# Two mixers and an MLP on one core: rotary products moved from GpSimd to VectorE, gates by tanh at later places, attention values beside the next scores, and four groups of unread transposes

## The chip, the cores and the metric

The kernel runs on one core of a Trainium2 chip. The metric is the device time of one execution in microseconds (us); lower is better. The engines are named as in the profile: PE (TensorE, with its weight loads as PEld), DVE (VectorE), ACT (ScalarE), POOL (GpSimd) and SP (the queue that issues the weight transfers).

## The reference, cut to what matters

Everything is float32, 256 tokens of width 2048. Two blocks follow one another.

```python
# first block
u = rms_norm(h, norm_mix_w);  z = u @ w_in           # 2048 x 11264
y_a = rms_norm(hgrn2_scan(...), hg_norm_w) * silu(hg)
y_b = chunk_band_attention(aq, ak, av, rel_bias)     # 16 heads of 64
merged = sigmoid(gates_a) * (y_a @ w_branch_a) + sigmoid(gates_b) * (y_b @ w_branch_b)
h = h + merged @ w_out
h = h + square(relu(rms_norm(h, norm_mlp_w) @ w_up)) @ w_down
# second block, 16 meta tokens ahead of the 256
qa, ka, va, ga, qb, kb, vb, gb = split(rmsnorm(h) @ w_in_2)   # 2048 x 6656
ya = attention(rope(rmsnorm(qa)), rope(rmsnorm(ka)), va) * silu(ga)      # 8 heads of 128
yb = rmsnorm(softmax(s1) @ vb - lam * softmax(s2) @ vb, sub_g) * (1 - lambda_init) * silu(gb)
h = h + rmsnorm(concat(ya, yb) @ w_out_2, post_norm_g)
```

`rope(x)` is `x * cos + turned(x) * sin`, per head.

## The kernel before, in words

Every projection is a stream of **chunks**: a chunk is 256 rows by 512 columns of a weight matrix. SP brings it into `raw` (four slots), ACT copies it rounded into `whi` (`split_hi`, L857), DVE writes the rest into `wlo` (`split_lo`, L1240), and PE multiplies it in three products, high by high, high by low, low by high. In the transposed form (`chunk_t`, L430) that is 24 matmuls of 256 columns, in the natural form (`chunk_n`, L442) 12 of 512. Eight chunks (k = 0 to 7) make one **group** of 512 output columns: `g` counts the 22 groups of the first projection, `j` the 13 of the second mixer's. Two sets of PSUM banks (banks 0-1 and 2-3) alternate between groups; banks 4 to 7 are for everything else.

All orders are written out by hand. Each engine has its own loop over the same chunks, and what is called "side work" here is inserted behind chunk k of group g. In the loops of ACT and DVE the place (g, k) begins with the split of chunk k+4, which waits until PE has finished chunk k, so these two engines enter place (g, k) when PE leaves chunk k. Each engine works strictly in its written order: an instruction that waits holds all that stand behind it, the splits included.

The places that the change touches:

- **First attention** (from `G_ATT` = 16). Eight pairs of heads, one every `PAIR_STEP` = 5 chunks: `att_scores` at the pair's place (PE L570, L572), exponentials one chunk later on ACT (L975), their inverse and product on DVE two chunks later (L1448), `att_turn` four chunks later (six transposes, PE L578), `att_copy` on ACT (L982), and `att_values` six chunks later (PE L589, L591). Pair j+1's scores stand at five.
- **HGRN output** (group `G_HGOUT` = 14): four copies on ACT at k = 2 to 5, four squares on POOL, `hg_squares` on PE behind k = 6 (L556), `hg_root` on ACT at k = 7.
- **First gates** (g = 14 to 21): at the end of the group DVE scales the PSUM set into `gates` (L1369) and ACT, at the end of its own group, waits for that and applies Sigmoid (L938).
- **Second mixer.** `rope_squares` (PE L696), `rope_root` (ACT), `rope_turn_halves` (PE L706), `rope_sin` (DVE L1588) for n = 0, 1, 2, and then `rope` on POOL: times cos, plus the sine part, times the inverse root (L1882, L1885, L1888). Units of attention run one per chunk from j = 6 on (place `pos` = 8(j-6)+k): `scores`, `weights_turn` three places later (L745), `values` four later (L758). For the gate groups (j = 9 to 12) DVE scales the set (L1619), ACT applies Sigmoid (L1105), and DVE, which waits for it, multiplies (L1621); POOL later multiplies this into the attention's output (L1902, L1909).

## Time and profile before

| | |
|---|---|
| median of 3 runs | 1920.42 us (1920.09 to 1922.02) |
| the profiled execution | 1919.19 us, its span 1917.4 us |
| PE busy | 1889.7 us, 99% of the span |
| DVE, ACT, POOL busy | 1101.7, 914.2, 178.9 us |
| granted TensorE clock, mean | 0.997 |
| the chain that ended last | PE 94%, DVE 3%, ACT 2%, issue 1% |

The span is measured from the first to the last instruction; 1.8 us of the execution lie around it. PE's matmuls overlap one another in the records, so its busy share says nothing of its speed: what counts is the time from one matmul's start to the next one's start, and the places where PE idles. A row of the chain gives start, length, engine, what is written, line and number of instructions; dividing length by number in a long row gives that distance.

### The profile page before, as it was taken

What the parts mean: (1) busy time and instruction counts of PE and PEld (TensorE: products, weight loads), DVE (VectorE), ACT (ScalarE), POOL (GpSimd) and SP (SyncE); (2) the same over time, 40 slices, a digit from 0 to 9 for tenths busy, and PEclk for the clock granted to TensorE, in tenths of its full rate; (3) what the DMA queues carried; (4) which work ended last, traced back from release to release, by engine and by line L of the source; (5) the groups of instructions that cost most, each with busy time, mean ns of one, the idle gap of its engine ahead of it and who ended that gap; (6) DMA issues with size and microseconds to landing.
All of it is one profiled execution on the core that took longest, in us unless ns stands there. A gap on an engine that the chain in (4) does not pass through costs nothing.

```text
span 1917.4 us, 33984 instructions
## 1 busy us (share of the span) xinstructions
PE 1889.7 (99%) x13468; PEld 1752.5 (91%) x13468; DVE 1101.7 (57%) x1265; ACT 914.2 (48%) x1189; POOL 178.9 (9%) x135
## 2 busy tenths in 40 slices
PE   9999999999999999999999999999999999998998
PEld 9989998999999889988998899899889998888986
DVE  6655766466655555554545545554566457766664
ACT  6534444565644455443443344344454354655543
POOL 2001331401000100000010000000010000031000
PEclk9999999999999999999999999999999999999999
DMA  8665656566565656666656666566555554444454
GB/s 272 191 180 171 185 179 177 152 193 177 171 220 186 208 187 177 196 199 189 196 187 198 190 195 194 190 183 202 188 185 173 175 170 133 116 136 144 133 187 143
DMA packets 176435, 346.49 MB, mean 181 GB/s; under 512 B 10976, under 2 KB 11184, under 8 KB 175776
## 3 DMA queue, kind: packets, MB, share of 16 engines
q1 hardware_dynamic: 174176, 337.76, 57.0%
q0 software_dynamic: 2128, 6.82, 1.4%
q8 instruction: 102, 1.67, 0.3%
q14 instruction: 29, 0.24, 0.0%
HBM read 342.44 MB, written 2.10 MB: 180 GB/s over the span
## 4 chain that ended last, share of the span: by engine, by line
PE 94%; DVE 3%; ACT 2%; issue 1%; DMA 0%; SPq 0%; POOL 0%; DVEq 0%; ACTq 0%
PE ps L430 56%; PE ps L442 32%; DVE wlo L1240 1%; ACT whi L857 1%; PE ps L758 1%; PE ps L527 1%; PE ps L745 1%; PE ps L722 0%; PE ps L460 0%; DMA x_nat<-in_x_dram 0%; PE ps L733 0%; PE ps L578 0%; PE ps L696 0%; DVE p L1652 0%; PE ps L570 0%
## 5 line engine op out<-in xcount | busy, mean ns | idle before, releaser
L1240 DVE TENSOR_TENSOR wlo<-raw,whi 128x1024 fp32r<-128x1024 f32 x631 | 804.1, 1280 | 719.3 <-ACT whi L857 718.3
L857 ACT ACTIVATE whi<-raw 128x1024 fp32r<-128x1024 f32 x631 | 664.1, 1058 | 872.6 <-PE ps L430 545.1
L430 PE MATMUL ps<-xhi,whi 128*128 128x256 f32 (+1 forms) x1984 | 567.3, 286 | 0.0
L430 PE MATMUL ps<-xhi,wlo 128*128 128x256 f32 (+1 forms) x1984 | 555.4, 280 | 0.0
L430 PE MATMUL ps<-xlo,whi 128*128 128x256 f32 (+1 forms) x1952 | 546.8, 280 | 0.0
L430 PEld LDWEIGHTS ps<-xhi,whi 128*128 128x128 f32 x1984 | 375.0, 189 | 10.0 <-issue 7.6
L430 PEld LDWEIGHTS ps<-xhi,wlo 128*128 128x128 f32 x1984 | 373.8, 188 | 0.0
L430 PEld LDWEIGHTS ps<-xlo,whi 128*128 128x128 f32 x1952 | 368.8, 189 | 1.5 <-issue 0.7
L430 PE MATMUL ps<-x2hi,whi 128*128 128x256 f32 x1024 | 282.8, 276 | 0.0
L430 PE MATMUL ps<-x2lo,whi 128*128 128x256 f32 x1024 | 282.7, 276 | 0.0
L430 PE MATMUL ps<-x2hi,wlo 128*128 128x256 f32 x1024 | 282.7, 276 | 0.0
L430 PEld LDWEIGHTS ps<-x2lo,whi 128*128 128x128 f32 x1024 | 192.2, 188 | 0.2
L430 PEld LDWEIGHTS ps<-x2hi,whi 128*128 128x128 f32 x1024 | 192.2, 188 | 0.2
L430 PEld LDWEIGHTS ps<-x2hi,wlo 128*128 128x128 f32 x1024 | 192.2, 188 | 0.0
L442 PE MATMUL ps<-whi,xlo 128*128 128x512 f32 x256 | 100.8, 394 | 0.0
L442 PE MATMUL ps<-whi,ya_lo 128*128 128x512 f32 x256 | 100.8, 394 | 0.0
L442 PE MATMUL ps<-whi,yb_lo 128*128 128x512 f32 x256 | 100.8, 394 | 0.0
L442 PE MATMUL ps<-whi,xhi 128*128 128x512 f32 x256 | 100.8, 394 | 0.0
L442 PE MATMUL ps<-wlo,ya_hi 128*128 128x512 f32 x256 | 100.3, 392 | 0.0
L442 PE MATMUL ps<-wlo,xhi 128*128 128x512 f32 x256 | 100.2, 392 | 0.0
L442 PE MATMUL ps<-wlo,yb_hi 128*128 128x512 f32 x256 | 100.2, 392 | 0.0
L442 PE MATMUL ps<-whi,ya_hi 128*128 128x512 f32 x256 | 99.7, 390 | 0.0
(357 smaller groups left out, 2220.6 us busy)
## 6 DMA issues: line engine op xcount, KB each, us to landing
raw<-in_w_in_dram SPq DMA_DIRECT2D x279, 512.0 KB, 3.8
raw<-in_w_up_dram SPq DMA_DIRECT2D x128, 512.0 KB, 3.8
raw<-in_w_down_dram SPq DMA_DIRECT2D x128, 512.0 KB, 3.7
raw<-in_w_out_dram SPq DMA_DIRECT2D x64, 512.0 KB, 4.0
raw<-in_w_branch_a_dram SPq DMA_DIRECT2D x16, 512.0 KB, 4.2
raw<-in_w_branch_b_dram SPq DMA_DIRECT2D x16, 512.0 KB, 4.1
x_nat<-in_x_dram SPq DMA_DIRECT2D x4, 512.0 KB, 7.0
rel<-in_rel_turned_dram POOLq DMA_DIRECT2D x8, 256.0 KB, 4.4
```

The lines of the kernel that those rows point to most:

```text
L430: ins = mm(outs[b], w[:, k % SLOTS, j, cols], v, start=start, stop=last and j == CK - 1 and i == 2, skip_group_check=True)
L442: ins = mm(ps[:, 2 * s + t, :], v[:, kt, toks], w[:, k % SLOTS, j, :], start=first and j == 0 and i == 0, stop=last and j == CK - 1 and i ...
L527: ins = mm(misc[:, hd // 4, (hd % 4) * P:(hd % 4 + 1) * P], k_both[:, hd, :], spread(qp[:, hd, 0:1], *both_tiles), start=True, stop=True)
L745: ins = nc.tensor.transpose(ps[:, 6, i * P:(i + 1) * P], p[:, i * P:(i + 1) * P], ident[:])
L758: ins = mm(ps[:, 7, 0:P], l, r, start=i == 0, stop=i == 2)
L857: f(whi[:, k % SLOTS], raw[:, k % SLOTS], ACT.Copy).then_inc(whi_ready, 1)
L1240: tt(wlo[:, k % SLOTS], raw[:, k % SLOTS], whi[:, k % SLOTS], ALU.subtract).then_inc(wlo_ready, 1)
```

## The change

It does five things.

1. First attention: `att_values` moves from six chunks behind its scores to five, directly ahead of the next pair's scores.
2. The gates of both mixers use tanh in place of the sigmoid (sigmoid(x) = (1 + tanh(x/2))/2; the factors of a half go into instructions that exist). In the first mixer `gate_tanh` stands on ACT at k = 2 of the next group. In the second, DVE only scales at the group's end and does the rest (`gate_out`) at k = 3 of the next group. `subg` moves from the gate into the copies behind `b_turn`.
3. `rope` and the products of gate and output move from POOL to DVE, each step at a place of its own (`ROPE_STEPS`). POOL keeps nothing in the second mixer but a memset and a DMA.
4. Some places move by one chunk: `hg_squares` and `hg_root`, `values_turn` and its copies, the third rope's squares and turn, `b_turn`.
5. `shift_phase`: three 128x128 transposes whose output nobody reads, at four places: behind (g = 15, k = 2), behind the last `att_values` (g = 21, k = 0), and at pos 20 and 30 of the second mixer.

```diff
+ROPE_FROM = (41, 65, 74)
+ROPE_STEPS = ((45, 54, 56, 58), (69, 70, 71, 71), (78, 85, 86, 87))
-POS_BT = 26
+POS_BT = 27
@@ PE
+            def shift_phase(bank, rows):
+                for i in range(3):
+                    nc.tensor.transpose(ps[:, bank, i * P:(i + 1) * P], rows(i), ident[:])
...
-                    if k == 6 and g == G_HGOUT:
+                    if k == 7 and g == G_HGOUT:
                         hg_squares()
+                    if k == 2 and g == G_HGOUT + 1:
+                        pe.wait_ge(hg_sd, 4)
+                        shift_phase(4, lambda i: acc[:, i, :])
                     at = NC * (g - G_ATT) + k
-                    for part, late in ((att_values, 6), (att_turn, 4), (att_scores, 0)):
+                    for part, late in ((att_values, 5), (att_turn, 4), (att_scores, 0)):
                         if pair_at(at - late) is not None:
                             part(pair_at(at - late))
+                    if at == PAIR_STEP * (AH // 2):
+                        shift_phase(5, lambda i: prob[:, 0, i * P:(i + 1) * P])
...
+                if pos in (POS_B + B_UNITS + 3, POS_BT + 3):
+                    if pos == POS_BT + 3:
+                        pe.wait_ge(bn_copied[0], 2)
+                        pe.wait_ge(bn_copied[1], 2)
+                    shift_phase(6, lambda i: kb[:, 4 * (i % 2), 0:P])
@@ ACT, first mixer
-                elif g >= 14:
-                    act.wait_ge(set_free[s], g // 2 + 1)
-                    v = gates[:, 4 * (g - 14):4 * (g - 14) + 4, :]
-                    f(v, v, ACT.Sigmoid).then_inc(gate_done, 1)
+            def gate_tanh(g):
+                act.wait_ge(set_free[g % 2], g // 2 + 1)
+                v = gates[:, 4 * (g - 14):4 * (g - 14) + 4, :]
+                f(v, v, ACT.Tanh, scale=0.5).then_inc(gate_done, 1)
...
+                    if g >= 15 and k == 2:
+                        gate_tanh(g - 1)
@@ DVE, branches: three instructions keep their number
-                tt(part_a[:], pset(0), gates[:, bass.ds(4 * n, 4), :], ALU.mult).then_inc(set_free[0], 1)
+                stt(out=part_a[:], in0=gates[:, bass.ds(4 * n, 4), :], scalar=1.0, in1=pset(0), op0=ALU.add,
+                    op1=ALU.mult).then_inc(set_free[0], 1)
@@ DVE, second mixer
+            def rope(n, step):
+                s = ROPE_SETS[n]
+                w = TM if n == 0 else T
+                nb = 2 if n == 0 else 4
+                v, r, q = qg[:, 0:nb, 0:w], qrot[:, 0:nb, 0:w], qsq[:, 0:nb, 0:w]
+                if step == 0:
+                    dve.wait_ge(nr_rot, n + 1)
+                    src = ps[:, 2 * s:2 * s + 2, 0:TM] if n == 0 else pset(s)
+                    tt(r, src, spread(sin_t[:], [0, nb], [1, w]), ALU.mult).then_inc(set_free[s], 1)
+                if step == 1:
+                    own(tt(v, v, spread(cos_t[:], [0, nb], [1, w]), ALU.mult))
+                if step == 2:
+                    dve.wait_ge(set_free[s], rope_free[n])
+                    own(tt(v, v, r, ALU.add))
+                if step == 3:
+                    dve.wait_ge(nr_rs, n + 1)
+                    tt(ka[:] if n == 0 else qa[:, 4 * (n - 1):4 * n, :], v, q, ALU.mult).then_inc(nr_done, 1)
...
-                tt(dst, pset(s), rows(4, T), ALU.mult).then_inc(g_raw, 1)
+                stt(out=dst, in0=pset(s), scalar=0.5, in1=rows(4, T), op0=ALU.mult, op1=ALU.mult).then_inc(g_raw, 1)
+                if j == G_IN2 - 1:
+                    gate_out(j)
+            def gate_out(j):
...
                 dve.wait_ge(e_sig, N_E1 + g + 1)
-                stt(out=dst, in0=pset(s), scalar=subg[:] if g < 2 else 1.0, in1=dst, op0=ALU.mult,
-                    op1=ALU.mult).then_inc(set_free[s], 1)
+                stt(out=dst, in0=pset(s), scalar=1.0, in1=dst, op0=ALU.add, op1=ALU.mult).then_inc(set_free[s], 1)
+                y, done = (ob, bn_y) if g < 2 else (oa, an_y)
...
+                tt(y[:, half, :], y[:, half, :], dst, ALU.mult).then_inc(done, 1)
...
+                    if j >= 10 and k == 3:
+                        gate_out(j - 1)
@@ POOL: rope(0), rope(1), rope(2) and the four products with ob and oa are gone
```

**PE at one place of the first attention.** Ahead of these rows and behind them stand matmuls of L430. Before, a pair's scores are followed by a whole chunk and only then come the values of the pair ahead:

```order
L570 MATMUL ps<-ak,aq 128x256 x2
L572 MATMUL ps<-ak,aq 128x128 x2
L430 MATMUL ps<-xhi,whi 128x256
...
L430 MATMUL ps<-xhi,wlo 128x256
L589 MATMUL ps<-prob_t,av 64x256 x2
L591 MATMUL ps<-prob_t,av 64x128 x2
L430 MATMUL ps<-xhi,whi 128x256
```

Now (L596 and L598 are the values, L577 and L579 the scores):

```order
L596 MATMUL ps<-prob_t,av 64x256 x2
L598 MATMUL ps<-prob_t,av 64x128 x2
L577 MATMUL ps<-ak,aq 128x256 x2
L579 MATMUL ps<-ak,aq 128x128 x2
```

The values have moved up by one chunk, so PE leaves and enters the stream of chunks twice per pair instead of three times.

**ACT from the third to the fourth pair.** L857 is the split, L938 the gate, L975 the exponentials, L982 the copies. Before:

```order
L982 ACTIVATE prob_t<-ps 128x384 x2
L857 ACTIVATE whi<-raw 128x1024
L938 ACT_TABLE_LOAD
L938 ACTIVATE gates<-gates 128x1024
L857 ACTIVATE whi<-raw 128x1024
L975 ACT_TABLE_LOAD
L975 ACTIVATE prob,rsum<-prob,nm 128x128
L975 ACTIVATE prob,rsum<-prob,nm 128x256
```

The same stretch now (L874 the split, L1001 the copies, L994 the exponentials, L957 the gate):

```order
L1001 ACTIVATE prob_t<-ps 128x384 x2
L874 ACTIVATE whi<-raw 128x1024 x2
L994 ACTIVATE prob,rsum<-prob,nm 128x128
L994 ACTIVATE prob,rsum<-prob,nm 128x256
L994 ACTIVATE prob,rsum<-prob,nm 128x128
L994 ACTIVATE prob,rsum<-prob,nm 128x256
L1005 ACTIVATE yb_hi<-ps 128x256
L874 ACTIVATE whi<-raw 128x1024 x2
L957 ACTIVATE gates<-gates 128x1024
```

The gate has left the place between two splits ahead of the exponentials, and both table loads are gone. Over the whole program ACT has 17 table loads in place of 36.

**DVE at pos 39, the last place of group j = 10, in the second mixer.** Before, L1637 is the maximum of a unit and L1619, L1621 the gate:

```order
L1637 TENSOR_REDUCE nm<-ps 128x1
L1638 TENSOR_SCALAR nm<-nm 128x1
L1619 TENSOR_TENSOR gb<-ps,row_s 128x1024
L1621 SCALAR_TENSOR_TENSOR gb<-ps,subg,gb 128x1024
L1240 TENSOR_TENSOR wlo<-raw,whi 128x1024
```

Now L1688 is the maximum, L1624 the last step of the third rope, L1655 the gate's scaling, L1262 the split:

```order
L1688 TENSOR_REDUCE nm<-ps 128x1
L1689 TENSOR_SCALAR nm<-nm 128x1
L1624 TENSOR_TENSOR qa<-qg,qsq 128x1024
L1655 SCALAR_TENSOR_TENSOR gb<-ps,row_s 128x1024
L1262 TENSOR_TENSOR wlo<-raw,whi 128x1024
```

The instruction that waited for ACT is gone from here, and a rope step stands ahead of the one that ACT waits for.

## Rows read from the trace of the kernel before

**Rows 1.** Waits of PE, whole run: us in total, times, longest us:

```profile
PE ps L745 <- DVE p L1652: 6.9, 3, 4.5
...
PE ps L578 <- DVE prob L1448: 2.0, 1, 2.0
PE ps L696 <- ACT qsq L1098: 1.8, 1, 1.8
PE ps L570 <- ACT prob_t L982: 1.2, 2, 1.1
PE ps L684 <- DVE v_meta L1580: 1.2, 1, 1.2
...
PE ps L556 <- POOL o_hg L1845: 1.0, 1, 1.0
...
PE ps L758 <- DVE oa L1658: 0.9, 2, 0.5
```

**Rows 2.** Timeline of ACT, first attention: start us, us, instruction, idle before:

```profile
453.46 1.06 ACT L938 ACTIVATE gates<-gates 128x1024 f32<-128x1024 f32 x1 [4.46 <-DVE gates L1369]
...
455.48 1.28 ACT L975 ACT_TABLE_LOAD   x1
```

**Rows 3.** Chain that ended last, 396 to 472 us: start us, us, what:

```profile
461.83 1.56 PE ps L578 x6
463.39 3.79 PE ps L430 x24
```

**Rows 4.** The same chain over the whole run and from 520 us:

```profile
521.96 8.68 PE ps L430 x72
...
531.30 5.46 PE ps L430 x48
...
537.56 107.61 PE ps L430 x912
...
912.12 87.07 PE ps L430 x768
```

**Rows 5.** Timeline of PE around one `att_values`:

```profile
415.80 0.28 PE L430 MATMUL ps<-xhi,wlo 128*128 128x256 f32 x1
416.01 0.65 PE L589 MATMUL ps<-prob_t,av 128*64 128x256 f32 x4
...
416.81 0.38 PE L430 MATMUL ps<-xhi,whi 128*128 128x256 f32 x1
417.03 0.28 PE L430 MATMUL ps<-xlo,whi 128*128 128x256 f32 x1
```

**Rows 6.** Timeline of PE, three transposes between two chunks:

```profile
1812.49 0.49 PE L745 MATMUL ps<-ident,p 128*128 128x128 f32 x3
...
1812.93 0.28 PE L430 MATMUL ps<-xlo,whi 128*128 128x256 f32 x1
```

**Rows 7.** Timelines of DVE, POOL and ACT, 1679 to 1740 us:

```profile
1717.79 1.22 DVE L1588 TENSOR_TENSOR qrot<-ps,sin_t 128x1024 f32<-128x1024 f32 x1
1719.48 6.50 DVE L1240 TENSOR_TENSOR wlo<-raw,whi 128x1024 fp32r<-128x1024 f32 x2 [0.47 <-ACT whi L857]
...
1721.63 3.27 POOL L1888 TENSOR_TENSOR qa<-qg,qsq 128x1024 f32<-128x1024 f32 x1
...
1727.69 1.03 ACT L1105 ACTIVATE ps<-gb 128x1024 f32<-128x1024 f32 x1 [4.11 <-DVE gb L1619]
```

**Rows 8.** Chain that ended last, 1560 to 1822 us:

```profile
1736.55 3.81 PE ps L430 x24
...
1809.82 2.83 PE ps L430 x24
1812.98 2.83 PE ps L430 x24
```

**Rows 9.** Timeline of DVE, 1755 to 1770 us:

```profile
1765.00 2.06 DVE L1652 TENSOR_SCALAR p<-p,rinv 128x272 f32<-128x272 f32 x1
```

**Rows 10.** Busy us (x instructions) of PE, PEld, DVE, ACT, POOL in one stretch:

```profile
1720.00:1822.00 102.00, 94.17 (x764) 91.80 (x762) 65.40 (x113) 52.60 (x84) 14.95 (x6) 0.98 0.45 139
```

More of the change, by code:

```diff
@@ L276, in program @@
         vt_t, vt_c = [sem("vt_t0"), sem("vt_t1")], [sem("vt_c0"), sem("vt_c1")]
-        nr_ev, nr_ss, nr_sd, nr_rs, nr_rot, nr_sin, nr_cos, nr_done = [sem(n) for n in (
-            "nr_ev", "nr_ss", "nr_sd", "nr_rs", "nr_rot", "nr_sin", "nr_cos", "nr_done")]
+        nr_ev, nr_ss, nr_sd, nr_rs, nr_rot, nr_done = [sem(n) for n in (
+            "nr_ev", "nr_ss", "nr_sd", "nr_rs", "nr_rot", "nr_done")]
         u_s, u_nm, u_exp, u_p, u_t, u_pt, u_pv, u_o = [sem(n) for n in (
@@ L817, in _ @@
                     chunk_t(c0, k, CK * k, xh, xl, outs, TM if kv else T, k == 0, k == NC - 1, shared=not kv)
-                    if j == 5 and 2 <= k <= 6:
-                        values_turn(2 * (k - 2))
-                        values_turn(2 * (k - 2) + 1)
-                    for n, jn in enumerate((5, 8, 9)):
-                        if j == jn and k == 1:
+                    if j == 5 and k >= 3:
+                        values_turn(2 * (k - 3))
+                        values_turn(2 * (k - 3) + 1)
+                    for n, first in enumerate(ROPE_FROM):
+                        if NC * j + k == first:
                             rope_squares(n, ROPE_SETS[n])
-                        if j == jn and k == 4:
+                        if NC * j + k == first + 3:
                             rope_turn_halves(n, ROPE_SETS[n])
@@ L1004, in _ @@
                         hg_copy(k - 2)
-                    if g == G_HGOUT and k == 7:
+                    if g == G_HGOUT + 1 and k == 0:
                         for i in range(4):
@@ L1021, in _ @@
                 evac_in(g)
+            gate_tanh(G_IN - 1)
             with act.Fori(0, 4) as n:
@@ L1027, in _ @@
                 act.wait_ge(br_m, n + 1)
-                f(uhi[:, bass.ds(4 * n, 4), :], both[:], ACT.Copy).then_inc(br_hi, 1)
+                f(uhi[:, bass.ds(4 * n, 4), :], both[:], ACT.Copy, scale=0.5).then_inc(br_hi, 1)
             def h_squares(n, free, done, into):
@@ L1104, in evac_in2 @@
                     act.wait_ge(g_raw, g + 1)
-                    f(pset(set_of(j)), dst[:, 4 * (g % 2):4 * (g % 2) + 4, :], ACT.Sigmoid).then_inc(e_sig, 1)
+                    f(pset(set_of(j)), dst[:, 4 * (g % 2):4 * (g % 2) + 4, :], ACT.Tanh).then_inc(e_sig, 1)
             def values_copy(b):
@@ L1159, in side @@
                     f(ob[:, 4 * i:4 * i + 2, :], ps[:, 4 + 2 * i, :].rearrange("p (x c) -> p x c", x=2),
-                      ACT.Copy).then_inc(bn_copied[0], 1)
+                      ACT.Copy, scale=subg[:]).then_inc(bn_copied[0], 1)
             def y_upper(mixer, i, src, ready, done):
@@ L1188, in _ @@
                             f(uhi[:, kt, :], xhi[:, kt, 0:T], ACT.Copy).then_inc(hi_packed, 1)
-                    if j == 5 and 3 <= k <= 7:
-                        values_copy(2 * (k - 3) + 1)
+                    if 4 <= NC * (j - 5) + k <= 8:
+                        values_copy(2 * (NC * (j - 5) + k - 4) + 1)
                     if j >= J_B:
                         side(NC * (j - J_B) + k)
-                    for n, jn in enumerate((5, 8, 9)):
-                        if j == jn and k == 2:
+                    for n, first in enumerate(ROPE_FROM):
+                        if NC * j + k == first + 1:
                             rope_root(n, ROPE_SETS[n])
@@ L1580, in values_copy @@
                 nc.vector.tensor_copy(v_meta[0:META, b, :], ps[0:META, 4 + b % 4, T:T + P]).then_inc(vt_c[0], 1)
[L1582 to L1588 removed]
+            rope_free = (SETS_BEFORE_2 + 4, need2[7] + 1, need2[8] + 1)
+            def rope(n, step):
[15 more added lines that the diff above has]
+                    tt(ka[:] if n == 0 else qa[:, 4 * (n - 1):4 * n, :], v, q, ALU.mult).then_inc(nr_done, 1)
             def rows(n, w):
@@ L1675, in b_norm @@
                     dve.wait_ge(bn_t, i + 1)
-                    nc.vector.tensor_copy(ob[:, 4 * i + 2:4 * i + 4, :],
-                                          ps[:, 5 + 2 * i, :].rearrange("p (x c) -> p x c", x=2)).then_inc(bn_copied[1], 1)
+                    ts(ob[:, 4 * i + 2:4 * i + 4, :], ps[:, 5 + 2 * i, :].rearrange("p (x c) -> p x c", x=2), subg[:],
+                       None, ALU.mult).then_inc(bn_copied[1], 1)
             def side(pos):
@@ L1713, in _ @@
                             nc.vector.tensor_copy(dst, xlo[:, kt, 0:T]).then_inc(lo_packed, 1)
-                    if j == 5 and 3 <= k <= 7:
-                        values_copy(2 * (k - 3))
-                    for n, jn in enumerate((5, 8, 9)):
-                        if j == jn and k == 5:
-                            rope_sin(n, ROPE_SETS[n])
+                    if 4 <= NC * (j - 5) + k <= 8:
+                        values_copy(2 * (NC * (j - 5) + k - 4))
                     if j >= J_B:
                         side(NC * (j - J_B) + k)
+                    for n, places in enumerate(ROPE_STEPS):
+                        for step, place in enumerate(places):
+                            if NC * j + k == place:
+                                rope(n, step)
+                    if j >= 10 and k == 3:
+                        gate_out(j - 1)
                     if j == G_IN2 - 1 and k in (2, 4):
```

51 lines of the change are left out of this document (13 added, 38 removed).

## The prediction

> **What bounds the kernel now.** I read the page first. PE is busy for 99% of the span, and the chain is 94% PE. The chip is not waiting for weights: the waits of PE name no transfer after the start. So time can come only from PE: from where it idles, or from how closely its matmuls follow one another.
>
> For the first I read the waits of PE [rows 1]. Look at the totals: DVE's `p` 6.9 us, `prob` 2.0, ACT's `qsq` 1.8, `prob_t` 1.2, `v_meta` 1.2, POOL's square 1.0, `oa` 0.9. Together that is 15.0 us in eleven waits, all around attention side work that this change touches.
>
> For the second I read long rows of the chain [rows 4]. The same 256-column matmul of L430 comes every 87.07/768 = 113.4 ns in the MLP, but every 107.61/912 = 118.0 ns from 537.56 us on, with nothing between the matmuls and no wait. PE thus has two distances for one instruction, 4.6 ns apart, and keeps one for a hundred microseconds. In the short rows the distance changes at side work: 8.68/72 = 120.6 ns behind an `att_values` (entry included), 5.46/48 = 113.8 ns behind the next six transposes. I call them the close and the wide distance.
>
> Then I read why ACT and DVE are late. In the timeline of ACT [rows 2] the gate at 453.46 us stood idle for 4.46 us: ACT had reached its group's end and waited for DVE to scale the last sums. Behind it on ACT stand a split, a table load of 1.28 us and the pair's exponentials; DVE's product waits for these, and PE's six transposes for DVE. The second mixer has the same figure at its gate groups [rows 7]: ACT idle 4.11 us ahead of its sigmoid. There DVE is held too: two splits take 6.50 us where one such instruction alone takes 1.22 us, while POOL's rope is at work (3.27 us for one product). At 1765.00 us a product of 272 columns takes 2.06 us [rows 9] while POOL multiplies.
>
> **The change part by part.**
>
> *HGRN squares one chunk later.* PE waited 1.0 us for POOL's fourth square [rows 1]. A chunk is 24 x 113.4 ns = 2.7 us, more than the wait, so it goes: **-1.0**. `hg_root` then has two more chunks before the first unread transposes wait for it.
>
> *First gates.* `gate_tanh` at k = 2 finds the scaling long done; it no longer stands between the split and the exponentials at a group's end, and the order shows no table load. Both waits of the first attention, 1.2 and 2.0 us, go. The 2.0 us wait had a wake: its six transposes took 1.56 us [rows 3], against some 0.11 us each elsewhere, so 0.9 us more; and the chunk behind took 3.79 us in place of 2.7, 1.1 us more. **-5.2** in all. ACT gives up 19 table loads, which cover nothing on the path besides. What is late next: the exponentials of one pair now share their place with a gate (at = 26), 1.06 us more on ACT, with more than two chunks until PE asks; nothing.
> The Trainium skill ("ScalarE: Activation LUTs", *Table sets: the hidden batching unit*) puts exp and tanh in one set, and its section *What ACT_TABLE_LOAD costs* asks about 2.7 us for each switch with its drain. The row shows 1.28 us and no drain; by the page's figure the loads would weigh twice as much, which changes no term, since only the waits count.
>
> *Values beside the next scores.* Going from the stream to `att_values` took 416.01 - 415.80 = 0.21 us, and from its first matmul behind to the second 417.03 - 416.81 = 0.22 us [rows 5], each 0.113 us in the stream. One entry and one exit less per pair saves 0.10 + 0.11 = 0.2 us, seven times: **-1.4**. The values now wait for copies made one chunk earlier; the scores at that place wait for the same copies already, so no new wait.
> Six stretches of three chunks behind values run wide, as the row at 521.96 us does [rows 4], at 72 x 4.6 ns = 0.33 us each; a seventh is the long one below. Behind scores the same chain mostly runs close. With scores last at the shared place: **-1.9** (bounds 0 to -2.0).
>
> *Unread transposes.* Three of them between two chunks: from the first to the second matmul behind is 1812.93 - 1812.49 = 0.44 us [rows 6], less 0.11 that belongs to the stream, so 0.33 us each time, 1.3 us for four. That is certain. What they return is a matter of the distance. At the second place stand the 912 matmuls at the wide distance: 912 x 4.6 ns = 4.2 us. The trace shows six transposes of `prob` against the identity, the same instruction, turning wide into close (8.68/72 to 5.46/48, [rows 4]). It also shows three of `p` turning nothing: 2.83 us per 24 ahead and behind [rows 8]. I take the first, because at this place they follow other side work and read the same tile: **-4.2 + 0.3**. At the first place six chunks remain to be turned, 0.7 - 0.3: **-0.3**. At the two places in the second mixer a handful of chunks: 0 (from +0.7 to -0.7).
>
> *Values' transposes.* They and their copies move a chunk away from `rope_root`, which with two table loads held ACT: **-1.2**, the whole wait for `v_meta`.
>
> *Third rope a chunk later, second rope on DVE ahead of the scaling.* PE waited 1.8 us for the squares of `qg`, behind DVE and POOL. DVE now does three steps of 1.22 us [rows 7] at 70 and 71, the scaling follows, and PE asks one chunk later: **-1.8**.
>
> *Gate groups of the second mixer.* The wait of 4.5 us (of 6.9) has POOL's hold on DVE, the wait for the sigmoid and the table load in its chain. Gone, DVE leaves the end of the group some 4 us earlier. The chunk behind it took 3.81 us in place of 2.83 [rows 8]: 1.0 more. I leave 0.2 us for what stays: **-5.3**. The other waits at the two later boundaries are 6.9 - 4.5 = 2.4 and 0.9 us. At one of them (j = 10) a rope step of 1.22 us now stands ahead of the scaling for which ACT waits, so I leave 1.2 us there: **-2.1**.
> DVE receives nine rope steps and four products, 13 instructions; those from 1720 us on are three and four of 1.22 us, 8.5 us. DVE was busy for 65.4 of those 102 us [rows 10]: they fit, and POOL's hold goes.
>
> *At nothing:* the branch products and `subg` (an instruction of the same size for another, on engines with idle time); `b_turn` a chunk later (nobody asks until pos 31).
>
> Sum: 1.0 + 5.2 + 1.4 + 1.9 + 3.9 + 0.3 + 1.2 + 1.8 + 5.3 + 2.1 = 24.1 us. The profiled execution took 1919.2 us, 1.2 below the median of 1920.4, and its waits are what I took away; 1920.4 - 24.1 = **1896.3 us**.
>
> **The rivals.**
>
> *The transposes turn nothing at the second place.* For it: the three of `p` above. Then the 4.2 us stay: 1900.5 us.
> The Trainium skill ("TensorE: Matmul & The Clock Gate", *Wait — 56ns, not 53.3ns?*) gives a warm matmul one distance, its columns over 2.4 GHz and a fixed 2.5 ns; by it no transpose could change anything. Two distances for one shape in the rows contradict it.
>
> *The waits move.* DVE holds more, and ACT still waits for its scaling at each group's end. If half of what the second mixer's gate groups and ropes give (1.8 + 5.3 + 2.1 = 9.2, so 4.6) comes back as waits of L758 and L745, it is 1900.9 us. Against it: DVE's idle third.
>
> *Slower: the wrong distance for the rest.* The distance persists. Every group of transposes ahead of the MLP left the close one in this trace, but if the new history leaves the wide one, 3,072 matmuls of `x2` and 960 of the second projection lose 4.6 ns each, 18.5 us, the 1,536 of 512 columns some 7 us at the same step, and the 4.2 us stay: 1896.3 + 29.7 = 1926 us. It decides once more than 24.1 us, some 5,200 matmuls, run wide. Eight transposes ahead of the MLP stand unchanged, so I hold it for unlikely.
>
> *No effect.* Waits return in full and the transposes fail: around 1919 us.
>
> **How the numbers follow.** The sum 0.54; transposes turn nothing 0.26; waits move 0.12; no effect 0.04; slower 0.04. The likeliest case has a range of its own from 1892 (the second mixer's wide chunks turn as well, no wait is left) to 1899. For 8 in 10 I take 1890 to 1903: it holds the first three cases but for their tails. A measurement of this kernel can tell about 0.2%, 3.8 us, from no change: faster 0.92, same 0.04, slower 0.04.
>
> **What would show it.** In the chain after, the row of 912 or so matmuls before the output projection should be near 103.4 us, not 107.6. The waits of PE should have no `prob`, `prob_t`, `qsq`, `v_meta` and no 4.5 us; L745 and L758 together below 2 us. ACT's idle ahead of the first gates should be gone, POOL idle from 1570 us. In the first attention no chunk should take 3.8 us. Wrong it would be by new waits of `nm`, or of a set that the gate frees three chunks later, or by long rows of 118 ns where there were 113.4.

## The result, and the profile after

The changed kernel took 1899.83 us (median of 4 runs, 1897.56 to 1900.73), the kernel before on the same chip 1920.26 us. The ratio is 0.9894, with a 95% interval from 0.9882 to 0.9906: 1.1% faster. The forecast was 1896.3 us, from 1890 to 1903. The profiled execution took 1897.56 us with a span of 1895.8, at a granted clock of 0.999.

I read the waits of PE first. Each row is an engine and line, what it waited for, the total in us, how often, and the longest:

```profile
PE ps L490 <- DMA mix_rows<-in_norm_mix_w_dram: 3.0, 1, 3.0
PE ps L770 <- DVE oa L1709: 1.8, 2, 1.5
PE ps L475 <- DMA x_nat<-in_x_dram: 0.9, 2, 0.7
PE ps L734 <- DVE nm L1686: 0.6, 2, 0.5
```

Against [rows 1], `p`, `prob`, `prob_t`, `qsq`, `o_hg` are gone and `v_meta` has 0.2 us left. What grew is the wait of the values for `oa`, with 1.5 us at the boundary behind group j = 10. (Line numbers are new: the stream's L430 and L442 are now L432 and L444, scores L577 and L579, values L596 and L598, the first mixer's turn L585, the unread transposes L495, the second mixer's values L770, the splits L874 and L1262.)

Then the chain, at one pair of the first attention, at the second place of the unread transposes, and at the output projection (start, us, what, instructions):

```profile
425.45 0.66 PE ps L585 x6
426.11 2.74 PE ps L432 x24
428.85 0.58 PE ps L596 x4
429.43 0.22 PE ps L598 x4
429.65 0.63 PE ps L577 x4
430.28 0.22 PE ps L579 x4
430.50 11.51 PE ps L432 x96
...
528.97 0.48 PE ps L495 x3
529.45 106.09 PE ps L432 x936
...
1800.29 87.91 PE ps L444 x384
```

Here is both the part that came out as forecast and the part that did not. The long row is now at 106.09/936 = 113.3 ns, the close distance, where [rows 4] had 118.0. But the 96 matmuls behind the shared place of values and scores take 11.51/96 = 119.9 ns with their exit: all four chunks wide. I had expected them close.

ACT's timeline around the fourth gate, the one that [rows 2] shows before:

```profile
455.83 1.06 ACT L874 ACTIVATE whi<-raw 128x1024 fp32r<-128x1024 f32 x1 [1.62 <-PE ps L432]
456.79 1.04 ACT L957 ACTIVATE gates<-gates 128x1024 f32<-128x1024 f32 x1
458.66 1.06 ACT L874 ACTIVATE whi<-raw 128x1024 fp32r<-128x1024 f32 x1 [0.82 <-PE ps L432]
459.62 0.85 ACT L1001 ACTIVATE prob_t<-ps 128x384 f32<-128x384 f32 x2
```

The gate stands right behind a split, with no idle time ahead of it and no table load behind.

To place the gains I took, in each trace, the time from the first matmul of one chunk to the first of a later one. Chunks are counted through the program: 112 to 119 is g = 14, 120 to 175 are the groups of the first attention and the one ahead, 176 to 239 the branches and their output, 240 the MLP, and j = 0 of the second mixer begins at 496. The last row runs from chunk 600 to the end of the span. These sums are worked out from the starts of the traces' matmuls, in us; they serve for the experiments too.

```
chunks              before changed  e12     e1      e3      e4      e6      e11
0-40   start        113.65  114.70  113.76  113.86  114.92  116.39  116.78  113.60
112-120 (squares)    31.96   30.19   30.19   30.19   30.19   31.96   30.19   30.19
120-176 (attention) 183.20  177.72  177.72  178.17  177.45  177.99  175.97  176.25
176-240 (branches)  181.57  177.60  177.60  181.57  177.60  181.57  177.60  177.60
240-536             825.73  825.73  825.97  825.74  825.74  825.75  825.73  825.74
536-552 (j=5,6)      60.73   59.78   59.60   59.58   59.59   61.16   59.61   59.67
568-576 (j=9)        30.05   28.22   28.21   28.22   28.58   30.34   28.22   28.21
576-584 (j=10)       36.31   29.54   29.54   29.55   29.54   35.96   29.54   29.53
584-592 (j=11)       34.60   34.20   34.31   34.20   34.20   34.69   34.29   33.00
592-600 (j=12)       29.65   28.10   28.09   28.10   28.30   29.63   28.30   28.30
600-632 (output)     95.64   95.65   95.65   95.66   97.35   95.64   97.36   97.36
```

Between the first two columns the sum of the gains is 21.6 us: 1.8 at the squares, 5.5 in the attention, 4.0 in the branches, 1.0 at j = 5 and 6, 10.6 from j = 9 to 12, and 1.1 lost at the start, where nothing was changed. Of the 1.8 at the squares 0.4 come back in chunk 120, just behind that row: the squares stand a chunk later now, and the chunk behind them takes 3.23 us in place of 2.83. So they gave 1.4, and the attention 5.9.

### The profile page after: what moved, and what is told of

Same layout as the page of the kernel before. It is cut to its first block, busy times and chain, and to the rows that moved or that the text cites. A ratio compares the mean times of both kernels' runs of the same rounds, so it can differ in the third digit from the quotient of the medians.

```text
span 1895.8 us, 33990 instructions
## 1 busy us (share of the span) xinstructions
PE 1881.1 (99%) x13480; PEld 1746.7 (92%) x13480; DVE 1102.9 (58%) x1278; ACT 888.8 (47%) x1170; POOL 143.5 (8%) x122
## 4 chain that ended last, share of the span: by engine, by line
PE 98%; DVE 1%; ACT 0%; DMA 0%; issue 0%; SPq 0%; DVEq 0%; ACTq 0%
PE ps L432 59%; PE ps L444 32%; PE ps L770 1%; PE ps L534 1%; PE ps L734 1%; PE ps L757 0%; ACT whi L874 0%; DVE wlo L1262 0%; PE ps L462 0%; DMA x_nat<-in_x_dram 0%; PE ps L745 0%; PE ps L585 0%; PE ps L577 0%; PE ps L596 0%; PE ps L718 0%
## 5 line engine op out<-in xcount | busy, mean ns | idle before, releaser
L1262 DVE TENSOR_TENSOR wlo<-raw,whi 128x1024 fp32r<-128x1024 f32 x631 | 796.7, 1269 | 699.2 <-ACT whi L874 698.2
L874 ACT ACTIVATE whi<-raw 128x1024 fp32r<-128x1024 f32 x631 | 664.5, 1058 | 888.9 <-PE ps L432 561.7
L432 PE MATMUL ps<-xhi,whi 128*128 128x256 f32 (+1 forms) x1984 | 565.5, 285 | 0.2
L432 PE MATMUL ps<-xhi,wlo 128*128 128x256 f32 (+1 forms) x1984 | 554.8, 280 | 0.0
L432 PE MATMUL ps<-xlo,whi 128*128 128x256 f32 (+1 forms) x1952 | 546.0, 280 | 0.0
L432 PEld LDWEIGHTS ps<-xhi,whi 128*128 128x128 f32 x1984 | 374.2, 189 | 9.1 <-issue 6.5
L432 PEld LDWEIGHTS ps<-xhi,wlo 128*128 128x128 f32 x1984 | 372.8, 188 | 0.0
L432 PEld LDWEIGHTS ps<-xlo,whi 128*128 128x128 f32 x1952 | 367.5, 188 | 1.4 <-issue 0.7
L432 PE MATMUL ps<-x2hi,whi 128*128 128x256 f32 x1024 | 282.8, 276 | 0.0
L432 PE MATMUL ps<-x2lo,whi 128*128 128x256 f32 x1024 | 282.7, 276 | 0.0
L432 PE MATMUL ps<-x2hi,wlo 128*128 128x256 f32 x1024 | 282.7, 276 | 0.0
L432 PEld LDWEIGHTS ps<-x2lo,whi 128*128 128x128 f32 x1024 | 192.2, 188 | 0.2
L432 PEld LDWEIGHTS ps<-x2hi,whi 128*128 128x128 f32 x1024 | 192.2, 188 | 0.2
L432 PEld LDWEIGHTS ps<-x2hi,wlo 128*128 128x128 f32 x1024 | 192.2, 188 | 0.0
L444 PE MATMUL ps<-whi,ya_lo 128*128 128x512 f32 x256 | 100.8, 394 | 0.0
L444 PE MATMUL ps<-whi,yb_lo 128*128 128x512 f32 x256 | 100.8, 394 | 0.0
L444 PE MATMUL ps<-whi,xlo 128*128 128x512 f32 x256 | 100.8, 394 | 0.0
L444 PE MATMUL ps<-wlo,ya_hi 128*128 128x512 f32 x256 | 100.3, 392 | 0.0
L444 PE MATMUL ps<-wlo,yb_hi 128*128 128x512 f32 x256 | 100.2, 392 | 0.0
L444 PE MATMUL ps<-whi,xhi 128*128 128x512 f32 x256 | 100.2, 391 | 0.0
L444 PE MATMUL ps<-wlo,xhi 128*128 128x512 f32 x256 | 100.1, 391 | 0.0
L444 PE MATMUL ps<-whi,ya_hi 128*128 128x512 f32 x256 | 99.7, 390 | 0.0
```

The costliest lines, as they stand in the source:

```text
L432: ins = mm(outs[b], w[:, k % SLOTS, j, cols], v, start=start, stop=last and j == CK - 1 and i == 2, skip_group_check=True)
L444: ins = mm(ps[:, 2 * s + t, :], v[:, kt, toks], w[:, k % SLOTS, j, :], start=first and j == 0 and i == 0, stop=last and j == CK - 1 and i ...
L874: f(whi[:, k % SLOTS], raw[:, k % SLOTS], ACT.Copy).then_inc(whi_ready, 1)
L1262: tt(wlo[:, k % SLOTS], raw[:, k % SLOTS], whi[:, k % SLOTS], ALU.subtract).then_inc(wlo_ready, 1)
```

## The experiments

Twelve experiments follow, the last of them the changed kernel again. All times are medians of four or five runs each, and the kernel before was measured on the same chip: 1921.56 us for e1 to e4, 1920.62 for e5 to e8, 1920.37 for e9 to e12. Runs of one kernel spread over 1 to 5 us, of which e12 shows a part, so small effects are read from stretches of the trace and not from medians.

**e1: no unread transposes at the second place.**

```diff
-                    if at == PAIR_STEP * (AH // 2):
-                        shift_phase(5, lambda i: prob[:, 0, i * P:(i + 1) * P])
```

> The changed kernel without the three unread transposes at the second place (behind the last pair of the first attention); the other three places stay. Theory (PE keeps one of two distances between matmuls until side work turns it): the row of some 936 matmuls of L432 from about 529 us takes 118.0 ns each, 110.4 us, in place of 113.35 ns and 106.1 us, and may leave at the same stage; against the changed kernel 4.3 us more less 0.3 us for the three transposes, so +3.9 us, about 1903.7 us at the median. Rival (the distance came from something else in the new order, such as scores last at the shared place): the row stays at 113.4 ns and the kernel takes 0.3 us less, about 1899.5 us.

Measured: 1902.38 us (1901.08 to 1903.43), 0.9901 of before (0.9886 to 0.9916). The chain:

```profile
528.25 110.44 PE ps L432 x936
```

The same 936 matmuls take 118.0 ns each. The first mixer's end (120 to 240) is 4.4 us longer than in the changed kernel, three transposes saved included. Nothing else in the program differs. The theory holds: three unread transposes of some 0.3 us are worth 4.4 us. It holds in all fourteen traces: chunks 176 to 240 take 177.60 us in the ten with these transposes and 181.57 us in the four without. Whether another small piece of work there, or a pause of that length, would turn the distance as well was not tried. The MLP behind is close in both, so the harm ends at the next groups of side work.

**e2: none of the twelve.**

```diff
-                    if k == 2 and g == G_HGOUT + 1:
-                        pe.wait_ge(hg_sd, 4)
-                        shift_phase(4, lambda i: acc[:, i, :])
...
-                    if at == PAIR_STEP * (AH // 2):
-                        shift_phase(5, lambda i: prob[:, 0, i * P:(i + 1) * P])
...
-                if pos in (POS_B + B_UNITS + 3, POS_BT + 3):
...
-                    shift_phase(6, lambda i: kb[:, 4 * (i % 2), 0:P])
```

> The changed kernel with none of the twelve unread transposes. Theory: the first place turned nothing (-0.3 us), the second is worth 3.9 us net, the third turned the two to five chunks around the second rope (24 matmuls each at 4.6 ns, 0.2 to 0.6 us, about its own cost of 0.3), the fourth costs 0.3: together about +3.6 us against the changed kernel, 1903.4 us. Rival (none of them matters): 12 transposes of 0.11 us less, 1898.5 us. If the distance behind the whole mixer changes with the history, the long rows of the MLP would show 118 ns and the time would be tens of us more; the row of 3,072 tells that.

Measured: 1904.83 us (1901.15 to 1905.88), 0.9905 (0.9890 to 0.9921). Chunks 120 to 240 took 359.41 us against 359.74 in e1: the first place returned nothing there and cost its own 0.33. But around the third place the chain has this, with no transposes near:

```profile
1678.04 16.39 PE ps L432 x144
```

In the changed kernel the row at this place was 16.40 us for 144, close as well, and I had given the third place the credit. In e3, with the transposes in place, it took 16.96 us. So at the third place they decided nothing that these traces show. At the fourth they cost nothing: without them PE waits for `qrot`, and the chunk behind takes 3.77 us for 3.52.

**e3: values back in a gap of their own.**

```diff
-                    for part, late in ((att_values, 5), (att_turn, 4), (att_scores, 0)):
+                    for part, late in ((att_values, 6), (att_turn, 4), (att_scores, 0)):
...
-                    if at == PAIR_STEP * (AH // 2):
+                    if at == PAIR_STEP * (AH // 2) + 1:
```

> The changed kernel with each pair's values back six chunks behind (in the gap by themselves, one chunk after the next pair's scores), the unread transposes of the second place one chunk later with them. My prediction valued the shared place at 3.3 us (1.4 for entries and exits, 1.9 for wide stretches that turn close). After the trace of the changed kernel my theory is that a pair of stretches there runs wide all four chunks, 16.56 us a pair against 16.65 us: the shared place gives about 0.1 us a pair, so this version takes 0.8 us more than the changed kernel, about 1900.6 us, with the stretch behind scores close (113.4 ns) and that behind values wide (119 to 120 ns). Rival (the shared place gives what was predicted and something else, such as the tanh gates, took it back): +3.3 us, 1903.1 us, and chunks behind the tanh gate longer than their neighbours.

Measured: 1899.41 us (1898.12 to 1899.95), 0.9882 (0.9867 to 0.9897). One pair of its chain:

```profile
432.62 8.68 PE ps L432 x72
441.30 0.66 PE ps L585 x6
441.95 2.74 PE ps L432 x24
444.69 0.63 PE ps L577 x4
445.33 0.22 PE ps L579 x4
445.55 2.92 PE ps L432 x24
448.47 0.58 PE ps L596 x4
449.05 0.22 PE ps L598 x4
449.27 0.79 PE ps L432 x5
```

A pair takes 449.27 - 432.62 = 16.65 us against 16.55 of the changed kernel (430.50 to 447.05 in its chain). The shared place saves an entry and an exit (0.2 us) and pays with a fourth wide chunk (0.1 us): 0.1 us a pair, some 0.7 us in all, where I had put 3.3. By the medians the two kernels can't be told apart. Part of e3's good time is not of its edit: the transposes of the first place, the same in both and ahead of it, left the close distance here (16.34 us for 144) and the wide one in the changed kernel (16.96).

**e4: the kernel before, with only the first gates changed.**

```diff
-                elif g >= 14:
-                    act.wait_ge(set_free[s], g // 2 + 1)
-                    v = gates[:, 4 * (g - 14):4 * (g - 14) + 4, :]
-                    f(v, v, ACT.Sigmoid).then_inc(gate_done, 1)
...
+                    if g >= 15 and k == 2:
+                        gate_tanh(g - 1)
```

> The kernel before with one part of the change alone: the first attention's gates by tanh, at k = 2 of the chunk group behind, with the branch products scaled for it. Theory: the waits for the last transposes (1.2 and 2.0 us, with wakes of 0.9 and 1.1 us) are gone, -5.2 us against the kernel before: about 1915.1 us; PE's waits list neither prob nor prob_t. Rival (the waits come from the exponentials' other neighbours, and the gates only move): waits of 1 to 3 us on prob stay and it takes 1918 to 1920 us.

Measured: 1915.22 us (1914.61 to 1917.64), 0.9966 (0.9952 to 0.9980). PE's waits begin:

```profile
PE ps L745 <- DVE p L1659: 6.9, 3, 4.5
PE ps L488 <- DMA mix_rows<-in_norm_mix_w_dram: 3.0, 1, 3.0
PE ps L696 <- ACT qsq L1103: 2.2, 1, 2.2
```

`prob` and `prob_t` are not among them, all others are. The stretch 120 to 176 fell from 183.20 to 177.99 us: 5.2, the term of the prediction, wakes included. The edit is both the tanh, which needs no table load, and the later place; which of the two removes the waits was not tried.

**e5 and e6: one, or three, unread transposes behind the shared place of six pairs.**

```diff
+                    if pair_at(at) is not None and pair_at(at) >= 2:
+                        pe.wait_ge(at_y, pair_at(at) - 1)
+                        shift_some(3, 6 + pair_at(at) % 2)
```

(`shift_some(n, bank)` is n transposes of `ident` into a bank that nobody reads any more; e5 has 1 for 3.)

> The changed kernel with ONE more unread transpose behind the shared place (values of a pair and scores of the next) in each of six pairs. In the changed kernel the 96 matmuls behind that place run wide (11.51 us, 119.9 ns each with the exit). Theory (side work of transposes can turn the distance): if one turns it, 96 x 4.6 ns = 0.44 us a pair come back for some 0.2 us (entry and transpose), -1.4 us in all, the row near 11.1 us. Rival (the count is too small, or a phase decides): the row stays at 11.5 us and the version is 6 x 0.1 to 0.2 = 0.6 to 1.2 us slower.

> The same with THREE unread transposes at each of the six places, as many as at the second place of the change. Theory (three behind values turn wide into close, as at 529 us): rows of 96 at 11.1 us, 0.44 us back for 0.33 to 0.4 us each: within 0.7 us of the changed kernel either way. Rival (behind scores they turn nothing): rows of 11.5 us and 2.0 to 2.4 us slower than the changed kernel.

Measured: e5 1898.16 us (1897.40 to 1899.82), 0.9891 (0.9873 to 0.9909); e6 1897.35 us (1894.87 to 1899.87), 0.9880 (0.9860 to 0.9899). A row of each, of the 96 matmuls behind; e5 first:

```profile
446.49 11.31 PE ps L432 x96
```

```profile
431.71 0.48 PE ps L500 x3
432.19 10.91 PE ps L432 x96
...
448.14 0.48 PE ps L500 x3
448.62 1.39 PE ps L432 x12
```

One transpose leaves the row wide (117.8 ns) and, what I had not thought of, the six that follow no longer turn it either: attention takes 178.64 us, 0.9 more than in the changed kernel. Three leave it close (113.6 ns); a pair takes 16.43 us (432.19 to 448.62), and attention 175.97, 1.7 us less than in the changed kernel. Six pairs are 0.7 of that; the rest is the first place, which turned here. Turned, it is worth 1.0 us up to chunk 176: 176.69 us in e8 and e9 for 177.72 in the changed kernel, though their edits lie far behind. Half of it is the six chunks that follow, the other half is mostly the row behind the first shared place, which then takes 11.10 us in e8 in place of 11.51, without transposes of its own. What the shared place leaves thus depends also on what came before it. The medians alone would not have told e5, e6 and the changed kernel apart.

**e7: the second mixer's gates finished at the group's end.** **e8: three rope steps on POOL.**

```diff
                 stt(out=dst, in0=pset(s), scalar=0.5, in1=rows(4, T), op0=ALU.mult, op1=ALU.mult).then_inc(g_raw, 1)
+                dve.wait_ge(e_sig, N_E1 + g + 1)
+                stt(out=dst, in0=pset(s), scalar=1.0, in1=dst, op0=ALU.add, op1=ALU.mult).then_inc(set_free[s], 1)
```

```diff
@@ DVE: steps 1 to 3 of rope(n, step) are taken out; POOL gets them back
+                tt(v, v, spread(cos_t[:], [0, nb], [1, w]), ALU.mult).then_inc(nr_cos, 1)
+                tt(v, v, r, ALU.add).then_inc(nr_cos, 1)
+                tt(dst, v, q, ALU.mult).then_inc(nr_done, 1)
```

> The changed kernel with the second mixer's gates finished at the group's end again: DVE waits there for ACT's tanh and multiplies; only the product with the attention output stays at k = 3. Theory: the moved gate is worth most of the 5.3 us of the boundary j = 9 and of the 2.1 us of the later ones, but POOL's hold and the table loads are still gone, so DVE leaves the boundary some 2.5 us later than in the changed kernel: +3 to +5 us, with waits of PE for DVE's p or oa of 1 to 3 us at each gate boundary. Rival (the table loads and POOL's hold alone made the wait): +0 to +1 us and no wait above 1.5 us.

> The changed kernel with three of the four rope steps on POOL again (times cos, plus the sine part, times the inverse root); sine on DVE, gate products on DVE as in the change. Theory: the place of the squares of the third rope is a chunk later, so the 1.8 us wait for qsq stays gone, but POOL's product holds DVE again where they run side by side (two splits 6.50 us in place of 2.4 in the kernel before): +1 to +3 us from waits of PE at the gate boundaries j = 9 and j = 10. Rival (POOL's hold cost nothing on the path): the DVE steps gone from its way give the j = 10 wait of 1.5 us back, -1 us against the changed kernel.

Measured: e7 1898.01 us (1895.94 to 1899.84), 0.9884 (0.9866 to 0.9902); e8 1899.18 us (1898.41 to 1900.76), 0.9896 (0.9879 to 0.9914). In e7 group j = 10 takes 29.54 us, to the hundredth what it takes in the changed kernel, and j = 11 34.45 (+0.25). My theory of 3 to 5 us is wrong: once the rest is in place, where the gate is finished costs next to nothing. In e8 j = 10 takes 31.49 us (+1.95, of which 1.6 at the chunk with the wait and 0.3 in three later chunks that ran wide), and j = 11 32.99 (-1.2), since no rope step stands ahead of the scaling. Both the theory's loss and the rival's gain are there, and nearly cancel. Its waits:

```profile
PE ps L757 <- DVE p L1695: 1.4, 1, 1.4
...
PE ps L770 <- DVE oa L1701: 0.6, 2, 0.3
```

**e9: e7 and e8 together.** **e10: e7 with Sigmoid again**

```diff
-                    f(pset(set_of(j)), dst[:, 4 * (g % 2):4 * (g % 2) + 4, :], ACT.Tanh).then_inc(e_sig, 1)
+                    f(pset(set_of(j)), dst[:, 4 * (g % 2):4 * (g % 2) + 4, :], ACT.Sigmoid).then_inc(e_sig, 1)
```

> The changed kernel with two parts undone together: the second mixer's gates finished at the group's end (e7, which alone cost PE nothing: its waits stayed 1.6 and 0.5 us), and three rope steps on POOL (e8, which alone made group j = 10 longer by 1.95 us and j = 11 shorter by 1.2). Theory (the 4.5 us wait of the kernel before came from both at once, DVE slowed by POOL while it stands on the serial chain scale, activation, multiply): j = 10 grows by 4 us or more over the 29.5 us of the changed kernel, with a PE wait of 3 us or more. Rival (the two are additive and the rest of the 4.5 us was the table load and sigmoid): j = 10 at 31.5 us, a wait of 1.5 us.

> The changed kernel with the second mixer's gates at the group's end and with Sigmoid in place of Tanh there, which brings its table loads back (it so computes other gate values); rope and gate products stay on DVE. Theory (the table load of 1.28 us stands on the chain between scale and multiply, but without POOL's hold DVE has the slack): PE's waits grow by no more than 1.3 us at each of the three boundaries, together +1 to +3 us. Rival (the table loads made most of the 4.5 us wait): group j = 10 grows by 3 us or more over 29.5 us.

Measured: e9 1899.26 us (1896.81 to 1900.68), 0.9895 (0.9878 to 0.9911); e10 1900.53 us (1898.88 to 1901.36), 0.9896 (0.9880 to 0.9913). Group j = 10 takes 31.11 us in e9 and 30.92 in e10, with waits for `p` of 1.4 and 1.1 us. So POOL and the place together don't make the 4.5 us wait, nor do place and table loads: e9 decides against its theory and gives its rival's figures, but e10 takes away that rival's reason, the table load. DVE in e9, just ahead of the boundary:

```profile
1705.24 1.22 DVE L1616 TENSOR_TENSOR qrot<-ps,sin_t 128x1024 f32<-128x1024 f32 x1
1707.16 2.93 DVE L1262 TENSOR_TENSOR wlo<-raw,whi 128x1024 fp32r<-128x1024 f32 x1 [0.70 <-ACT whi L874]
...
1710.54 1.22 DVE L1647 SCALAR_TENSOR_TENSOR gb<-ps,row_s 128x1024 f32<-128x1024 f32 x1
```

and POOL at the same time:

```profile
1706.60 2.40 POOL L1934 TENSOR_TENSOR qg<-qg,qrot 128x1024 f32<-128x1024 f32 x1 [3.27 <-DVE qrot L1616]
1709.08 3.28 POOL L1937 TENSOR_TENSOR qa<-qg,qsq 128x1024 f32<-128x1024 f32 x1
```

Put beside [rows 7]: before, two splits lay under POOL's sum and product and took 6.50 us, here one does and takes 2.93. The third rope now begins a chunk later.

**e11: a version with both things that helped.** To e6, the same for the first of the seven pairs, and one table entry.

```diff
-ROPE_STEPS = ((45, 54, 56, 58), (69, 70, 71, 71), (78, 85, 86, 87))
+ROPE_STEPS = ((45, 54, 56, 58), (69, 70, 71, 71), (78, 84, 85, 86))
```

**e12: the changed kernel again**, with no edit.

> The changed kernel with three unread transposes behind the shared place of all seven pairs (e6 had six and turned the 96 matmuls behind to 11.0 us each), and the third rope's steps 1 to 3 one chunk earlier (84, 85, 86), so that its last step no longer stands ahead of the scaling at the boundary of j = 10. Theory: -1.2 us from the pairs (134 to 176), -1.2 us from the boundary (the 1.5 us wait of the values for oa falls below 0.3): about 2.4 us below the changed kernel, which runs in the same call. Rival: the step now stands ahead of another wait and the 1.5 us only moves: -1.2 us alone.

> The changed kernel itself once more. Theory (the distance behind the start is a lottery of the first transfers' times): of the stretches that do not differ between kernels, chunks 8 to 13, 13 to 32 and 32 to 40 take either 13.60, 52.98 and 21.97 us or up to 14.13, 54.99 and 22.40 us, and its single runs spread over some 3 us. Rival (the distances are fixed by the program): every stretch as in the first profile of this kernel, 14.13, 53.41 and 21.98 us, to 0.05 us.

Measured side by side: e11 1895.97 us (1895.56 to 1896.47), 0.9876 (0.9860 to 0.9893); e12 1898.43 us (1897.03 to 1898.69), 0.9889 (0.9872 to 0.9905). The slowest run of e11 is faster than the fastest of e12: 2.5 us by the medians, where 2.4 were expected. The boundary gave its part (34.31 to 33.00 us at j = 11), and so did the pairs (1.0 us from chunk 128 to 176). The rest of the match is luck: between the two traces the first place gave 0.5 us that no edit explains and the output lost 1.7, so that their spans are 1.5 us apart. Its waits:

```profile
PE ps L743 <- DVE nm L1695: 0.7, 2, 0.6
PE ps L779 <- DVE oa L1718: 0.6, 2, 0.3
```

All seven rows behind the pairs are at 10.91 us. e12 against the first trace of the same kernel: chunks 0 to 40 take 113.76 us and not 114.70, everything behind agrees within 0.25 us per row of the table. The chain at the start, of e12 and then of e2, whose program is the same up to chunk 120:

```profile
24.05 5.89 PE ps L432 x48
30.38 29.94 PE ps L432 x264
60.32 1.08 PE ps L484 x16
61.40 41.02 PE ps L432 x360
```

```profile
23.82 5.70 PE ps L432 x48
29.96 31.09 PE ps L432 x264
61.05 1.09 PE ps L484 x16
62.14 42.60 PE ps L432 x360
```

The row of 264 is close in one and wide in the other, and so is the row of 360, in the same instructions. Ahead of them PE waits for the first transfers. That these decide the distance is my reading; no run isolates it. The clock does not: it is 1.00 in both stretches.

## Why the prediction was right, and where its steps were off

The time lies within the stated range, but 3.5 us above the forecast and just outside the 1892 to 1899 of the likeliest case; e12, the same kernel, gave 1898.43. The waits went and the long row turned, as reasoned. Some terms were too large and others too small.

**The waits.** *First gates*: -5.2 forecast, 5.21 measured alone (e4). *Third rope*: -1.8 forecast, 1.83 at j = 9. *Values' transposes*: -1.2 forecast, 1.40 at j = 5 less some 0.4 at j = 6, 1.0 for both. *HGRN squares*: -1.0 forecast, 1.4 measured (chunks 112 to 121). I counted only the wait; the eight squares behind it also took 3.67 us in place of 3.43, and a wide chunk followed. Elsewhere (the first attention) I had added such wakes, here not.

**The wakes are the clock.** For two waits I priced slow rows behind them without saying what made them slow. The granted clock says it, in the trace of the kernel before (us; busy time of PE, PEld, DVE, ACT, POOL; then the granted clock):

```profile
461.50:467.20 5.70, 5.37 (x32) 4.89 (x32) 3.50 (x8) 1.23 (x3) 0.00 (x0) 0.70 0.63 184
1730.00:1740.30 10.30, 5.75 (x34) 5.32 (x34) 5.71 (x10) 4.43 (x8) 3.17 (x1) 0.83 0.53 151
```

From 462.10 to 465.50 us, and from 1735.30 to 1738.60, it is 0.50: 1.2 GHz, the lower of its two levels. Just before, PE had stood idle for 2.0 and for 4.5 us. An estimate of the loss is 0.30 x 5.70 = 1.7 us and 0.17 x 10.30 = 1.8 us, 3.5 of the 21.6 us that were gained. In the changed kernel the clock is 1.00 at both places, in e4 the second fall alone is left, and e8, e9 and e10, whose longest wait in the second mixer is 1.6 us, have none. A wait of 2 us does not always bring it: e4 waited 2.2 us for `qsq` at a granted clock of 1.00. But this part of the gain comes with the long wait, whichever part of the change shortens it.

**The boundaries of the gate groups.** Forecast 5.3 + 2.1 = 7.4; measured 6.77 + 0.40 + 1.55 = 8.7 at j = 10 to 12. The size is about right and 1.5 us stay at the boundary where I had left 1.2, for the reason given there: in the chain of the changed kernel the rope's last step (1.13 us) stands ahead of the scaling (1.15), and e11, with that step a chunk earlier, lost the wait:

```profile
1740.42 1.13 DVE qa L1624
1741.56 1.15 DVE gb L1655
...
1744.77 1.22 DVE wlo L1262
1745.99 0.21 DVE oa L1709
```

PE's values wait for `oa`, `oa` stands behind that split on DVE, and the split waits for ACT, which waits for the scaling of `gb`. Of the three reasons that I gave for the 4.5 us wait, DVE's wait for the sigmoid at the group's end carries little by itself: e7 brought it back for nothing, and together with Sigmoid and its table loads it was worth 1.4 us at j = 10 (e10). POOL's hold was 1.6 us there (e8, e9). Each was undone with the rest in place; what one of them alone would have saved in the kernel before was not measured. Some 1.8 us more are the clock. What is left of the 6.8 us, about 2, has no run of its own. The traces suggest the second split under POOL's hold: before, two splits took 6.50 us where two free ones take 2.4, so 4.1 us were lost, and in e9 it is 2.93 - 1.22 = 1.7 us. The 2.4 us between them would have gone because the third rope was moved a chunk. That is argued and not shown: moving only the third rope back was not tried.

**The unread transposes.** Forecast at the second place -4.2 + 0.3; e1 measured 4.4 net. The rival by which they turn nothing gave 1900.5 us, near the measured 1899.8, but it is refuted in its mechanism: its long row would be at 118 ns, and the row is at 113.3. The one number of the total would have misled here. The page "TensorE: Matmul & The Clock Gate" of the Trainium skill (*Wait — 56ns, not 53.3ns?*) has a single warm distance. The 264 matmuls at the start, 29.94 us in one run and 31.09 in another at a granted clock of 1.00 in both, have two. Each of these matmuls has a weight load of its own, so the rows show where the page's figure does not reach, not that it is wrong for matmuls without one. At the first place I expected -0.3: it is -0.7 when it turns (1.0 less its own 0.3) and +0.3 when it doesn't. It turned in five of the eleven traces that have it; the instructions ahead of it are the same in all of them, and what decides is open.

**The step that failed: values beside the next scores**, -1.4 and -1.9. I reasoned from which side work comes last at the shared place: scores alone are left close, values alone wide, so scores last should leave close. The group as a whole left wide, four chunks instead of three. The two terms together gave 0.7 us in place of 3.3. This is the largest miss. The profiled pair gained 21.6 us where the sum was 24.1: 2.6 are missing here, 1.1 at the start, where nothing was changed, 0.6 at the first place and 0.2 at the values' transposes, while the boundaries gave 1.3, the second place 0.5 and the squares 0.4 more than forecast; 0.2 stay unassigned. Between the medians the gain is 20.6 us (1920.42 to 1899.83), 1.0 less again, within the spread of the runs.

**The rivals of moved waits and of the wide distance behind the mixer** did not come: PE's waits after the start are 2.6 us in all, and the MLP's rows are at 113.4 ns in every trace. But the second of them has a small real form. The output projection's 384 matmuls of 512 columns took 87.91 us in seven of the fourteen traces and 89.61 in the other seven; the stretch 600 to 632 is 95.65 or 97.36 us. It is not the program at this place that differs, so it is what came ahead; e2, e3, e6, e7, e8, e10 and e11 lost 1.7 us there, and no experiment separates an effect of their edits from chance.

## What to carry to other kernels

Read the time from matmul to matmul in long undisturbed rows before calling a PE-bound kernel finished; if one instruction has two distances, look for what stands ahead of the row, and test a cheap group of unread transposes there. Judge it by that row, not by the total. A stall behind several engines is best costed from the place where it ends, and its price includes what the granted clock does behind it. Which part of the change removes it is told by undoing the parts one by one, and even that tells only what a part is worth beside the others: here one that looked responsible was free to undo.

## What the runs showed of the hardware that was not expected

- The same instructions run close or wide from one execution to the next: the first 40 chunks, which no edit touches, took between 113.4 and 116.8 us in fourteen traces, and 114.70 and 113.76 us in the two of the changed kernel. This can make up to 3.4 us between two runs of one kernel. It comes behind the first transfers; that their times decide it is not shown.
- Behind a wait of 2.0 us and one of 4.5 us PE ran at a granted clock of 0.50 for some 3.4 us each (kernel before).
- What three transposes do depends on more than their number. At the first place the same three left 144 matmuls at 16.96 us in six traces and at 16.34 in five. In the starts of single matmuls all eleven are wide ahead of them; the first transpose comes 118 or 119 ns behind the last matmul in the six that stay and 122 or 123 ns in the five that turn. One transpose behind the pairs never turned (six cases of e5), three did in all thirteen cases of e6 and e11.
- DVE's hold by POOL depends on the operands. While POOL multiplied (1709.08 to 1712.36 us in e9), the scaling with one input in PSUM took its usual 1.22 us; the split with both inputs in SBUF, which lay under POOL's sum (1706.60 to 1709.00) and the start of that product, took 2.93 in place of 1.22. The Trainium skill ("SBUF — State Buffer", *Who interferes with whom*) says that a DVE instruction with at most one input in SBUF, outside the two-port modes, doesn't contend with GpSimd, and that one with two contends with an instruction of GpSimd that reads SBUF. The rows agree with both.
